# Weight remainders by accumulating DMA, conv pads by ScalarE: a hybrid SSM and attention step on one core

## What is computed

```
proj = x @ w_in                          # z, xBC, dt, q, k, v, gates; D_MODEL = 1024
xbc  = silu(conv4(concat(conv_state, xBC)))   # depthwise, width 4, own carried state for each sample
y, h = ssd_chunked(x, dt, a, B, C, h0)   # 8 groups of 4 heads, chunks of 128 tokens, state 64 x 128 per head
y    = rmsnorm_per_group(y * silu(z)) * g
attn = dilated windows over q, k, v and the caches
x    = layernorm(alpha * x + (gate_ssm * (y @ w_ssm_br) + gate_attn * (attn @ w_attn_br)) @ w_o)
x    = layernorm(alpha * x + relu(x @ w_up)^2 @ w_down)
```

## Time and profile before

| | us |
|---|---|
| median of 3 runs | 2848.85 |
| lowest, highest | 2848.42, 2849.97 |
| the profiled execution | 2851.52 |
| its span | 2850.0 |
| busy in the span: PE, weight loads | 2635.8, 2477.2 |
| busy: DVE, ACT, POOL | 1245.4, 1067.2, 1082.8 |
| mean granted PE clock | 0.965 |

### The profile page before, as it was taken

The page is one execution under the profiler, slowest core; times in us unless marked ns, Lnnn a source line. Parts: engine busy times, 40 slices in busy tenths (PEclk is TensorE's granted clock), DMA queues, the critical chain, the costliest instruction groups (busy, mean ns, idle before and its releaser), DMA issues.

```text
span 2850.0 us, 53948 instructions
## 1 busy us (share of the span) xinstructions
PE 2635.8 (92%) x21376; PEld 2477.2 (87%) x21376; DVE 1245.4 (44%) x1916; ACT 1067.2 (37%) x1553; POOL 1082.8 (38%) x838
## 2 busy tenths in 40 slices
PE   7979899999799989999899898999997999999996
PEld 7956788888699989999899577888887999999996
DVE  4340677777611541021343407787774115310214
ACT  3251456555322253132242415555553222522323
POOL 4311344444334343344253014444433333443333
PEclk9999999999899999999999998999998999999998
DMA  4224233333222222222222242333331222222222
GB/s 140 82 101 155 85 111 137 108 127 123 73 86 86 84 67 89 89 89 88 69 91 80 103 148 95 125 121 125 105 135 67 86 85 84 72 84 88 89 89 76
DMA packets 67327, 280.53 MB, mean 98 GB/s; under 512 B 8369, under 2 KB 8433, under 8 KB 60737
## 3 DMA queue, kind: packets, MB, share of 16 engines
q1 hardware_dynamic: 51696, 184.31, 19.2%
q0 software_dynamic: 15440, 93.60, 9.1%
HBM read 248.81 MB, written 29.07 MB: 98 GB/s over the span
## 4 chain that ended last, share of the span: by engine, by line
PE 79%; DVE 9%; ACT 4%; POOLq 2%; issue 2%; POOL 1%; DMA 1%; DVEq 1%; ACTq 1%; SPq 0%
PE acc L417 21%; PE acc L418 21%; PE acc L420 20%; DVE region L1440 2%; POOLq L1790 2%; PE px L682 1%; PE acc L647 1%; PE px L740 1%; PE px L752 1%; DVE region L1558 1%; DVE region L1552 1%; PE acc L840 1%; PE acc L462 1%; PE px L609 1%; PE px L447 1%
## 5 line engine op out<-in xcount | busy, mean ns | idle before, releaser
L417 PE MATMUL acc<-xhi,whi 128*128 128x272 f32 x3552 | 999.2, 299 | 7.4 <-ACT big L952 3.9
L1692 POOL TENSOR_TENSOR wring_parts<-wring,whi 128x1024 fp32r<-128x1024 f32 x257 | 627.3, 2443 | 947.1 <-ACT whi L890 938.1
L418 PE MATMUL acc<-xlo,whi 128*128 128x272 f32 x3552 | 967.6, 291 | 0.0
L420 PE MATMUL acc<-xhi,wring_parts 128*128 128x272 f32 x3552 | 742.5, 290 | 0.0
L417 PEld LDWEIGHTS acc<-xhi,whi 128*128 128x128 f32 x3552 | 677.7, 191 | 29.9 <-issue 22.2
L890 ACT ACTIVATE whi<-wring 128x1024 fp32r<-128x1024 f32 x343 | 362.1, 1056 | 879.1 <-DMA wring<-in_wst 776.6
L418 PEld LDWEIGHTS acc<-xlo,whi 128*128 128x128 f32 x3552 | 677.2, 191 | 3.0
L420 PEld LDWEIGHTS acc<-xhi,wring_parts 128*128 128x128 f32 x3552 | 561.8, 190 | 0.0
L417 PE MATMUL acc<-region_parts,whi 128*128 128x272 f32 x1792 | 489.0, 291 | 15.2 <-DVE big_parts L1616 8.0
L418 PE MATMUL acc<-big_parts,whi 128*128 128x272 f32 x1536 | 419.3, 291 | 0.0
L420 PE MATMUL acc<-region_parts,wring_parts 128*128 128x272 f32 x1792 | 370.7, 288 | 0.0
(11 more groups left out here) (238 smaller groups left out, 2909.3 us busy)
## 6 DMA issues: line engine op xcount, KB each, us to landing
wring<-in_wst SPq DMA_DIRECT2D x343, 512.0 KB, 3.4
region<-scratch_ac POOLq DMA_DIRECT2D x16, 1088.0 KB, 6.5
region<-in_st POOLq DMA_DIRECT2D x16, 1024.0 KB, 5.3
out_stout<-region POOLq DMA_DIRECT2D x16, 1024.0 KB, 4.9
big<-in_kc POOLq DMA_DIRECT2D x16, 768.0 KB, 5.8
big<-in_vc POOLq DMA_DIRECT2D x16, 768.0 KB, 5.5
out_kv<-region POOLq DMA_DIRECT2D x2, 3264.0 KB, 11.3
region<-in_x SPq DMA_DIRECT2D x8, 272.0 KB, 5.2
```

Source lines behind the costliest of these rows:

```text
L417: nc.tensor.matmul(o, w_hi_, hi, start=first, stop=False)
L418: nc.tensor.matmul(o, w_hi_, lo, start=False, stop=False)
L420: mm = nc.tensor.matmul(out[:, 512 * h:512 * h + HT], w_lo_, parts(h)[0], start=False, stop=last)
L1692: pool.tensor_tensor(wlo[:, slot, :], whole[:, slot, :], whi[:, slot, :].bitcast(F32), ALU.subtract)\
```

## The change

- For 41 of the 170 units of each layer (`ADDED`: units 27 to 67, which ACT rounds in the steps that scan), ACT writes, behind the rounded part, its negative into `wlo` as well. POOL, in place of the subtraction, issues a transfer that reads the unit from HBM once more and adds it to `wlo` (`low_added`). `gemm` waits for a second count, `w_added`. The marks of the scan that held the halves back are gone. Unit 26 is now subtracted in the first step, and unit 68 in one piece.
- The four new sample columns of a pad are copied by ACT from PSUM in `evac`, ahead of the tile itself. The carried columns of all four tiles are put there by one POOL copy at the head of the step (`pad_states`), after the convs of the step before. `conv_init` waits for it with q = 0 alone.
- The last columns go out from `raw` itself, by one transfer (`store_tail`), and `tile(0)` of the next step waits for it. `cout` is gone.
- ACT drains behind every `tile`.
- DVE: conv(3) stands ahead of decay_states.

```
+ADDED = range(U_GRP + 6 + AHEAD, U_MRG + 2)
...
+def unit_of(L, u):
+
+    slot, use = unit(L, u)
+    same = [v for v in ADDED if v % SLOTS == slot]
+    return (slot, use, 16 * (L * len(same) + same.index(u) + 1)) if u in ADDED else (slot, use)
...
+                for j, (slot, use, *added) in enumerate(units):
                     pe.wait_ge(w_split[slot], use + 1)
+                    if added:
+                        pe.wait_ge(w_added[slot], added[0])
...
-                nc.scalar.activation(whi[:, slot, :], whole[:, slot, :], ACT.Copy).then_inc(w_hi[slot], 1)
...
+                hi = nc.scalar.activation(whi[:, slot, :], whole[:, slot, :], ACT.Copy)
+                if u in ADDED:
+                    act.drain()
+                    hi = nc.scalar.activation(wlo[:, slot, :], whi[:, slot, :].bitcast(F32), ACT.Copy, scale=-1.0)
+                hi.then_inc(w_hi[slot], 1)
...
+                if pad is not None:
+                    nc.scalar.activation(pad, acc[b][:, 512 + HT - TS:512 + HT].rearrange("p (b t) -> p b t", b=NB), func)
                 nc.scalar.activation(halves(out), two(acc[b]), func, **kw).then_inc(acc_free[b], 1)
...
-                        act.wait_ge(spad_ready, 4 * c + q + 1)
+                        if q == 0:
+                            act.wait_ge(spad_ready, c + 1)
...
+                            if k == 0:
+                                act.wait_ge(cout_st, 16 * c)
...
+                        act.drain()
...
                         norm_scale()
+                        conv(3)
                         decay_states()
-                        conv(3)
                         silu(3)
...
+            def low_added(L, u):
 
                 slot, use = unit(L, u)
+                pool.wait_ge(w_hi[slot], use + 1)
+                pool.dma_start(wlo[:, slot, :], row(A["wst"], L * UNITS + u, "u p n -> (u p) n").bitcast(F32R),
+                               accum_op=ALU.add).then_inc(w_added[slot], 16)
+                pool.sem_inc(w_split[slot], 1)
...
+                def pad_states(g):
 
                     c = L * GROUPS + g
+                    if g > 0:
+                        hold(pool, conv_done, 4 * c)
+                    pool.tensor_copy(raw[:, :, SAMPLE:RAWW].rearrange("p q (b t) -> p q b t", b=NB)[:, :, :, 0:PAD],
+                                     cst[:, 4 * g:4 * g + 4, :].rearrange("p q (b t) -> p q b t", b=NB))
                     pool.drain().then_inc(spad_ready, 1)
...
+                def store_tail(g):
+
+                    hold(pool, acc_free[3 % 2], read_of(L, T_GRP, 3 * g, 3))
+                    pool.dma_start(row(A["cout"], L * GROUPS + g, "o p q n -> (o p) q n"),
+                                   raw[:, :, SAMPLE - 35:SAMPLE]).then_inc(cout_st, 16)
```

More of the change, by code:

```diff
@@ L289, in build @@
         w_split = [sem(f"w_split{i}") for i in range(SLOTS)]
+        w_added = [sem(f"w_added{i}") for i in range(SLOTS)]
         w_used = [sem(f"w_used{i}") for i in range(SLOTS)]
@@ L822, in group @@
                         if g is not None:
-                            gemm(L, T_GRP, 3 * g, k, [unit(L, u + k, rounds)], x_parts, between)
+                            gemm(L, T_GRP, 3 * g, k, [unit_of(L, u + k)], x_parts, between)
                         elif k < 2:
-                            gemm(L, T_MRG, 0, k, [unit(L, U_MRG + k)], x_parts, between)
+                            gemm(L, T_MRG, 0, k, [unit_of(L, U_MRG + k)], x_parts, between)
                         else:
@@ L1050, in tile @@
                         out = raw[:, k, PAD:SAMPLE] if k < 4 else rawz[:, k - 4, :]
-                        evac(L, T_GRP, 3 * g, k, unit0 + k, rounds, out, ACT.Copy, scale=1.0 if k < 4 else 0.5)
+                        pad = (raw[:, k, SAMPLE:RAWW].rearrange("p (b t) -> p b t", b=NB)[:, :, PAD:] if k < 4 else None)
+                        evac(L, T_GRP, 3 * g, k, unit0 + k, rounds, out, ACT.Copy, pad, scale=1.0 if k < 4 else 0.5)
+                        act.drain()
                     def copy_y():
@@ L1798, in group @@
                         pool.memset(raw[:, :, 0:PAD], 0.0)
-                        for q in range(4):
-                            pad_of(g, q)
+                        pad_states(g)
+                        store_tail(g)
                         load_decay(g, L * GROUPS + g)
@@ L1804, in group @@
                         low(L, u + 4 + AHEAD)
+                        low(L, u + 5 + AHEAD)
                         return
@@ L1810, in group @@
                     if projects:
-                        hold(pool, cout_st, 16 * (L * GROUPS + g))
+                        pad_states(g)
                     last = U_GRP + 6 * gs + 5 + AHEAD
-                    for h in range(2):
-                        hold(pool, t_done, 5 * s + h + 1)
-                        low_half(L, last, h)
+                    if last in ADDED:
+                        low_added(L, last)
+                    elif not projects:
+                        low(L, last)
                     if projects:
-                        pad_of(g, 0)
-                        for h in range(2):
-                            hold(pool, t_done, 5 * s + h + 3)
-                            low_half(L, u + AHEAD, h)
-                        pad_of(g, 1)
-                        hold(pool, m_ready, 5 * s + 5)
-                        for h in range(2):
-                            low_half(L, u + 1 + AHEAD, h)
+                        low_added(L, u + AHEAD)
+                        low_added(L, u + 1 + AHEAD)
                     hold(pool, h_ready, 4 * s + 4)
@@ L1829, in group @@
                         load_decay(g, L * GROUPS + g)
-                        pad_of(g, 2)
-                        for h in range(2):
-                            low_half(L, u + 2 + AHEAD, h)
-                        pad_of(g, 3)
-                        hold(pool, rs_spread, s + 1)
-                        for h in range(2):
-                            low_half(L, u + 3 + AHEAD, h)
+                        low_added(L, u + 2 + AHEAD)
+                        store_tail(g)
+                        low_added(L, u + 3 + AHEAD)
                     hold(pool, h_st, 16 * s + 16)
@@ L1839, in group @@
                     if projects:
-                        hold(pool, post_ready, 4 * (L * GROUPS + g) + 4)
-                        for h in range(2):
-                            low_half(L, u + 4 + AHEAD, h)
+                        low_added(L, u + 4 + AHEAD)
                     hold(pool, ns_add, s + 1)
```

21 lines of the change are left out of this document (1 added, 20 removed).

## The result

The kernel after takes 2829.31 us (median of 11 runs, 2814.71 to 2839.51), the kernel before beside it 2849.46 (11 runs, 2842.23 to 2854.11). The ratio is 0.9925, 95% interval 0.9906 to 0.9945. It is faster by 20 us where 40 were forecast. That is inside the range (2786 to 2838) and outside the forecast's own (2798 to 2820). The runs of after lie 25 us apart. The profiled execution took 2832.83 us with a span of 2831.0: 19.0 less than before's 2850.0.

The account below looks back on a forecast made before the run. PE was taken as bound by waits for POOL, through ACT's late square, and slow clock. Terms -36.9 (twelve steps), -6.0 (first steps), -1.4 (group 0), +4 (POOL's issues) sum to -40.3 us, giving 2809 us; range 2786 to 2838.

Parts of the forecast that it names:

- what bound the steps: Scanning steps: PE waits 2.31 us at `rms` and 0.97 at the turn; the square is late through ACT's wait for POOL.
- the price of ACT's extra work: Between copy_y and the square: negative copy 1.05 us, pad copy 0.25, drains 0.17 each; together 1.6, ready 0.5 before gated_y.
- the order of DVE's tail: From `rms` to the turn: conv(3) ahead of decay_states, which covers ACT's tanh; turn wait about 0.6 us, not 0.97.
- the path behind `rms`: turn_y, y_carried, gated_y, square up to line 776: 0.50 of the 2.31 us wait stays, 1.8 goes.
- 4 us to spare: Transfer to unit u + 2 lands at 17 us after the turn; PE uses it at 21.3.
- Taken 0: Added DMA traffic, share rising from 0.35 to 0.51 to 0.67: later plain loads are covered, no cost.
- pad_states and its drain (0.5 to 5.6, median 0.9): POOL's work ahead of the transfer to unit u + 2, in us, with the drain priced from the trace of before.
- D: Rival: accumulating transfer to unit u + 2 late, PE idle at third `gemm`; at 14 us landing, 2861 us; chance 0.11.
- E: Rival: the wait only moves, conv_init(0) waits for POOL's drain behind pad_states; time as before, 2849 us; chance 0.03.
- C: Rival: ACT takes POOL's place, the square or conv_act(2) late by 1.45 us more a step; 2829 us; chance 0.20.
- POOL's issues, + 4 us: Six transfer issues a step at 0.55 us of POOL each; 0.3 us a step taken on DVE's path.
- Group 0, -1.4 us: conv_init(0) waited 2.44 us for pads; bounds 0 and -2.4 a layer, taken -0.7 a layer.

Follow-up runs that it names:

- run 2: Kernel after, with POOL's copy of the carried states in pad_states counted on the copy itself and not on a drain: 2806.11 us, 0.9850 of before.
- run 4: Kernel after with plain transfers in place of the accumulating ones (accum_op removed, output not the reference's), drain kept: 2803.35 us, 0.9843 of before.
- run 5: Kernel after with its drain kept, but pad_states and drain moved ahead of the load of the states: 2801.14 us, 0.9831 of before.
- run 10: Kernel after, pads copied ahead of the states' load and counted without drain, plus unit 24 made by an accumulating transfer: 2795.65 us, 0.9817 of before.

## Why the prediction was right or wrong

- **Right: what bound the steps.** ACT's wait for POOL made the square late, and with it gone `rms` waits 0.39 us (forecast 0.50) and the turn 0.45 (forecast 0.6). ACT stands ready 0.93 us before the square, 0.64 in one step of each layer, not 0.5. Without the drain a step takes 51.67 us in the mean (forecast 52.0), twelve of them 620.0 against 624, and the kernel 2806 us against 2809. So the price of ACT's extra work, the order of DVE's tail and the path behind `rms` were read rightly.
- **Wrong: "4 us to spare" on the way of unit u + 2.** The prediction's terms, beside the medians of the twelve later steps, in us after the turn. PE of after was ready for the unit at 21.6 (forecast 21.3).

| | forecast | after | run 2, no drain | run 4, no adding |
|---|---|---|---|---|
| load of the states issued | 6.3 | 9.3 | 9.4 | 8.6 |
| that load landed | 11.6 | 16.4 | 16.9 | 15.2 |
| transfer to unit u + 2 issued | not given | 17.6 | 10.4 | 16.5 |
| it landed | 17 | 23.1 | 20.0 | 20.2 |

- The first two terms carry 4.8 of the 6.1 us. The store of the states takes 8.0 us here and not 5.0, so the load starts 3.0 us later; the load itself adds 1.8. "Taken 0" for the DMA traffic holds for SP's loads (3.4 us before and after), not for those on POOL's own chain of store, load, drain and transfer. The transfer itself was sized rightly: 5.5 us at this place (forecast 5.3); the 6.8 of the page is the median of all 82.
- **Also wrong: "pad_states and its drain (0.5 to 5.6, median 0.9)".** Most of the 64 drains behind that median had no transfer in flight. In the new order each has a load of 1 MB issued right ahead of it, and its price is that load's landing, 7.1 us in the median. The prediction's sum happened to take the transfer as "served behind" the load, which is what the drain enforces, so pricing the drain rightly would have added only some 1.2 us to it. But it was not the queue that put them in series. Without the drain (run 2) the transfer is issued beside the load and lands 3.1 us earlier, just in time. With the longer store and load, the drain is what makes it late; run 5 keeps the drain, moves it ahead of the load, and gives the gain back.
- In the step shown above the same terms give the longest wait: turn at 1935.91, load issued at + 9.9, landed at + 18.2, drain ended at + 18.7, transfer issued at + 19.4, landed at + 26.5, with PE ready at + 21.6.
- **The prediction's own signs** say the same. Steps of 54.25 us are beyond the 53.5 at which it calls itself wrong, and D's sign is there (idle PE at the third `gemm`, a DMA as releaser), in a mild form: D's priced case, a transfer of 14 us, did not happen (10.1 at most in after). E's sign is there too, ACT's 59.2 us of waits for the drain at q = 0, but ACT has caught up by the square. That 2829 lies inside the range is luck: the range reaches that far for C, whose number it is, and C needs ACT late at the square, where ACT is on time.
- **The Trainium skill** ("Collectives: The Full Stack", The bandwidth ceiling) has a reducing transfer at about half the rate of a copy. Run 4 shows 6.8 us against 4.4, 1.55 times the landing and not twice, and 5.5 against 3.7 at unit u + 2. The direction agrees. The prediction's sentence that nothing in the sum would change leaned on 4 us to spare; as the store and the load really were, the adding decides whether PE waits (21.6 us with it, 0.98 without).
- **POOL's issues, + 4 us:** not seen. The issue takes 0.91 us and not 0.55, yet in run 2 the conv takes 2.7 us and the twelve steps save 40.9 us where the forecast had 36.9, which is these 4 us.
- **Group 0, -1.4 us:** the first turn came 2.6 us earlier in layer 1 and 0.4 earlier in layer 2, counted from the last turn of layer 1. conv_init(0) had waited for a drain here too, and POOL's first subtraction moved from beside conv(1) to beside conv(0), where it still costs some 2 us (run 10).
- **The runs' spread** of 25 us, against 2.5 in run 2, fits a wait that hangs on landings of 5.5 to 8.3 us. But there are eleven runs against four, the five of run 5 lie 12 us apart, and only one profile was taken of after, so this is not shown.

## What to carry to other kernels

Ahead of moving work off an engine, look at what its waits are made of: here one semaphore moved from a drain to the copy itself gave 25 us, where three new mechanisms gave 20. In these traces a drain of GpSimd's behind its own transfer is a wait for that transfer, so count a copy on its own completion or put the drain ahead of the issue. If a change adds a second stream of transfers, do not price the transfers that stay by their old landings. And price an operation whose durations spread tenfold by its neighbours in the new order, not by its median.

## What the runs showed of the hardware that was not expected

- POOL's drain ended only when the transfer issued ahead of it had landed: in after it took 5.8 to 8.6 us and ended 0.5 us behind the landing in twelve steps, in before 26 drains ended 0.13 to 0.17 us behind one. With no such transfer in flight it took 1.25 us in the median (run 5).
- An accumulating transfer of 512 KB into SBUF landed in 6.8 us against 4.4 for a plain one, and its issue took 0.91 us of POOL against 0.54. The transfers of POOL's queue took 17.6% of the DMA engines' span with the adding and 14.5% without, for the same bytes.
- A second stream of loads left SP's loads at 3.4 us but lengthened the 1 MB load of the states from 5.3 to 6.9 us and their store from 4.9 to 7.9. Without the adding (run 4) they took 6.9 and 7.3.
- A transfer of POOL's issued about 1 us behind its 1 MB load did not wait for it to land: the two were in flight together, and the transfer landed 9.0 us after its issue in the median of twelve steps (run 2), against 5.5 where the load had landed first (after).
- A DVE operation with both inputs in SBUF stood still for as long as POOL's subtraction ran: conv 2.70 and 5.37 us, the last operation of silu 0.18 and 1.28.
